# Latent attention of a two-block transformer kernel: keys before queries, and a per-row scale in the exponential

## The reference, cut to what matters

```python
lat = h @ w_in
cq, ckv, k_pe = jnp.split(lat, [Q_LORA, Q_LORA + KV_LORA], axis=-1)
q = (rmsnorm_2(cq, q_norm) @ w_q_up).reshape(B, S, N_HEADS_2, QK_HEAD)
kv = (rmsnorm_2(ckv, kv_norm) @ w_kv_up).reshape(B, S, N_HEADS_2, QK_NOPE + V_HEAD)
k_nope, v = jnp.split(kv, [QK_NOPE], axis=-1)
k = jnp.concatenate([k_nope, jnp.broadcast_to(k_pe[:, :, None, :], ...)], axis=-1)
q = rope_tail(rmsnorm_2(q, q_head_norm), cos, sin)
k = rope_tail(rmsnorm_2(k, k_head_norm), cos, sin)
o = causal_attention(q, k, v)        # softmax(q k^T * QK_HEAD ** -0.5) v
return o.reshape(B, S, N_HEADS_2 * V_HEAD) @ w_out
```

## Time and profile before

| what | value |
|---|---|
| median of the runs | 2693.09 us (2692.44 to 2696.33, three runs) |
| profiled execution, its own time | 2700.57 us |
| its span in the profile | 2698.5 us |
| mean granted TensorE clock | 0.959 |
| latent attention stage, strip 2 to the output strips | 2042.1 to 2290.3 us of the span |

### The profile page before, as it was taken

One profiled execution on the slowest core, in us unless ns is written; L12 is line 12 of the kernel. 1 busy time (PEld: TensorE's weight loads), 2 busy tenths in 40 slices (PEclk: granted clock), 3 DMA queues, 4 the chain that ended last, 5 costly groups with the idle time before them and its releaser, 6 DMA issues.

```text
span 2698.5 us, 29334 instructions
## 1 busy us (share of the span) xinstructions
PE 2587.5 (96%) x10854; PEld 1803.9 (67%) x10854; DVE 1172.3 (43%) x1789; ACT 750.1 (28%) x1049; POOL 29.1 (1%) x24
## 2 busy tenths in 40 slices
PE   7989969999999699999999999999999999999999
PEld 2865533333333488888888888888887646888887
DVE  5765451222221644433644433544436546544432
ACT  3124321000101333322433322333223225433321
POOL 0000000000000300000000000000000000000000
PEclk9986879999999799999899999999999979999999
DMA  6650138999998133322232322333322200233332
GB/s 241 212 171 1 66 137 353 422 422 422 422 422 368 48 100 93 110 100 82 68 98 96 108 96 84 93 101 96 107 85 84 81 32 1 86 101 93 100 106 74
DMA packets 80858, 403.58 MB, mean 150 GB/s; under 512 B 8984, under 2 KB 9496, under 8 KB 55968
## 3 DMA queue, kind: packets, MB, share of 16 engines
q1 hardware_dynamic: 80800, 402.82, 40.8%
HBM read 400.69 MB, written 2.10 MB: 149 GB/s over the span
## 4 chain that ended last, share of the span: by engine, by line
PE 89%; DVE 5%; DMA 2%; ACT 2%; issue 1%; POOL 0%; SPq 0%; ACTq 0%; DVEq 0%; POOLq 0%
PE pb L900 21%; PE pb L901 20%; PE pb L902 20%; PE pb L1108 8%; PE pb L1134 4%; PE pb L1074 2%; PE pb L1095 2%; DMA stage<-in_w_in 1%; PE pb L996 1%; PE pb L1291 1%; PE pb L1009 1%; PE pb L1023 1%; PE pb L997 1%; DMA adaw<-in_w_ada 1%; PE pb L1281 1%
## 5 line engine op out<-in xcount | busy, mean ns | idle before, releaser
L1385 DVE TENSOR_TENSOR wL<-stage,wH 128x1024 fp32r<-128x1024 f32 (+2 forms) x303 | 393.6, 1300 | 821.2 <-ACT wH L539 821.1
L900 PE MATMUL pb<-hH,wH 128*128 128x512 f32 x1688 | 667.8, 396 | 25.7 <-DVE gf L1747 8.5
L901 PE MATMUL pb<-hL,wH 128*128 128x512 f32 x1688 | 660.2, 391 | 0.0
L902 PE MATMUL pb<-hH,wL 128*128 128x512 f32 x1688 | 659.8, 391 | 0.0
L539 ACT ACTIVATE wH<-stage 128x1024 fp32r<-128x1024 f32 (+2 forms) x303 | 337.3, 1114 | 892.5 <-PE pb L902 822.5
L900 PEld LDWEIGHTS pb<-hH,wH 128*128 128x128 f32 x1688 | 319.2, 189 | 103.8 <-issue 11.8
L901 PEld LDWEIGHTS pb<-hL,wH 128*128 128x128 f32 x1688 | 318.9, 189 | 67.6 <-issue 2.8
L902 PEld LDWEIGHTS pb<-hH,wL 128*128 128x128 f32 x1688 | 318.8, 189 | 67.4
L900 PE MATMUL pb<-gH,wH 128*128 128x512 f32 x704 | 273.9, 389 | 0.0
L901 PE MATMUL pb<-gL,wH 128*128 128x512 f32 x704 | 273.9, 389 | 0.0
L902 PE MATMUL pb<-gH,wL 128*128 128x512 f32 x704 | 273.9, 389 | 0.0
(11 more groups left out here) (271 smaller groups left out, 2271.5 us busy)
## 6 DMA issues: line engine op xcount, KB each, us to landing
ring<-in_experts SPq DMA_DIRECT2D x192, 1024.0 KB, 17.7
stage<-in_gate SPq DMA_DIRECT2D x88, 512.0 KB, 3.5
stage<-in_up SPq DMA_DIRECT2D x88, 512.0 KB, 3.5
stage<-in_down SPq DMA_DIRECT2D x64, 704.0 KB, 4.0
adaw<-in_w_ada SPq DMA_DIRECT2D x48, 512.0 KB, 5.5
stage<-in_w_in SPq DMA_DIRECT2D x18, 512.0 KB, 6.7
stage<-in_mla_in SPq DMA_DIRECT2D x9, 512.0 KB, 3.6
stage<-in_q_up SPq DMA_DIRECT2D x12, 384.0 KB, 3.0
```

The costliest lines, as they stand in the source:

```text
L900: pe.matmul(ps, lh, rh, start=first, stop=False)
L901: pe.matmul(ps, lh, rl, start=False, stop=False)
L902: return pe.matmul(ps, ll, rh, start=False, stop=last)
L1385: dve.tensor_tensor(wL[:, n % 2, 0:w], stage[:, n % STAGE, 0:w], wH[:, n % 2, 0:w], ALU.subtract).then_inc(strip_lo, 1)
```

## The change

It touches the latent attention stage only.

- **Order.** Latent strips come as key/value 6, 7, rotated key part 8, then query 0 to 5. Key strips come next, then the twelve query strips (rotated ones at places 0, 1, 6 and 7), then the value strips.
- **Query norms.** A query tile is no longer multiplied by any reciprocal. DVE copies plain tiles and multiplies rotated ones by their gain alone. The sums of squares of the raw queries go to four rows for heads 0 to 3 and 4 to 7, are copied out, turned by 4 small transposes (4 x 128 to 128 x 4), and joined on tokens x heads with the query latent's reciprocal (another 4 transposes): a table of 128 x 32 scales. The exponential takes a column of it as its scale, and the bias is the maximum times the same column.
- **Spreads.** Only the eight for keys are left; two follow each of query strips 3 to 6. Head sums follow each key head and each query strip, rotations 1 to 4 follow query strips 7 to 10. The gain of the queries' plain part is folded into the keys'.
- **Values** are made and taken in the four banks one by one, rather than by waiting for a whole strip.
- **Other.** Angles are worked out in two pieces at strips 2 and 3; the first strip of the output waits for each head's low half in turn, not for all; the second output strip's `hi` and `lo` move into the attention's first units; positions and the selection table are loaded after the fifth latent strip; semaphores, tile counters and banks are renumbered.

The diff, cut to its core:

```diff
-        NX, NCTX, NH2, NFIN, N1A, NMA, N2A, N1B, NMB, NQL, NKL, N2B = range(12)
+        NX, NCTX, NH2, NFIN, N1A, NMA, N2A, N1B, NMB, NKL, NQL, N2B = range(12)
+        LAT_ORDER = (6, 7, 8, 0, 1, 2, 3, 4, 5)
+        Q_ORDER = (0, 1, 4, 5, 6, 7, 2, 3, 8, 9, 10, 11)
+        K_BANKS = ((1, 3, bank(T_MIN + 7), bank(T_MIN + 8)), (1, 3, 7, 6))
+        V_BANKS = (1, 3, bank(T_MQ + 10), bank(T_MQ + 11))
+        def q_scale(h, b):
+            c = 32 + 16 * (h // 4) + 4 * b + h % 4
+            return qstat[:, c:c + 1]
...
# PE
-            for s in range(9):
-                whole(M_IN + s, T_MIN + s, KD, hH, hL, lows_of=LO0[NMB] if s == 0 else None)
-                if s == 0:
-                    norm_sum(NMB)
-                if s == KQ:
-                    norm_sum(NQL)
+            for j in range(9):
+                whole(M_IN + j, T_MIN + j, KD, hH, hL, lows_of=LO0[NMB] if j == 0 else None)
+                if j == 0:
+                    norm_sum(NMB)
+                if j == 3:
+                    norm_sum(NKL)
...
+            def head_sum(n):
+                pe.wait_ge(hq_sq, n + 1)
+                ...
+                if n == 9:
+                    pe.wait_ge(std_done, NQL + 1)
...
+            def qsum_turn(group):
+                pe.wait_ge(qsum_copied, group + 1)
+                for b in range(NB):
+                    mm = pe.transpose(pb[4 + group][:, 4 * b:4 * b + 4], qsum[group][:, b * P:(b + 1) * P], tab("ident", 4)[0:4, :])
+                if group == 0:
+                    pe.wait_ge(rstd_done, NQL + 1)
+                    for b in range(NB):
+                        mm = pe.transpose(pb[4][:, 16 + b:17 + b], rstd_q[0:1, b * P:(b + 1) * P], tab("ident", 1)[0:1, :])
+                mm.then_inc(qsum_turned, 1)
+
+            for m in range(4):
+                keys_of(0, m)
+            turn(0, krope[:, :])
+            head_sum(0)
+            for m in range(4):
+                keys_of(1, m)
+                head_sum(1 + m)
             for s in range(12):
...
+                queries(s)
+                if s < 2:
+                    head_sum(5 + 2 * s)
+                    head_sum(6 + 2 * s)
+                else:
+                    head_sum(7 + s)
+                if s == 1:
+                    norm_sum(NQL, at=4)
+                if 3 <= s <= 6:
+                    spread_rows(2 * s - 6)
+                    spread_rows(2 * s - 5)
+                if 7 <= s <= 10:
+                    turn(s - 6, qr[:, s - 7, :])
+                if s == 9:
+                    qsum_turn(0)
+            head_sum(19)
+            values_of(0, 0)
+            head_sum(20)
+            for i in range(1, 4):
+                values_of(0, i)
+            for i in range(4):
+                values_of(1, i)
+                if i == 1:
+                    qsum_turn(1)
...
-            pe.wait_ge(att_lo, NB + MH)
             for s in range(KD):
-                whole(M_OUT + s, T_MOUT + s, KD, oH, oL)
+                whole(M_OUT + s, T_MOUT + s, KD, oH, oL, heads_of=NB if s == 0 else None)
...
# ACT
             for s in range(12):
                 hi(M_Q + s + 2)
+                if s == 2:
+                    root(NQL, KQ * P, at=4)
+                    act.wait_ge(hq_summed, 9)
+                    act.activation(head_std[:, :], pb[5][0:MH, :], ACT.Sqrt, bias=eps[0:MH, 0:1], scale=1.0 / (NOPE + ROPE))\
+                       .then_inc(hq_std, 1)
...
-                act.activation(p, p, ACT.Exp, bias=stat[:, 16 + u % 4:17 + u % 4], scale=SCALE2,
+                act.activation(p, p, ACT.Exp, bias=stat[:, 16 + u % 4:17 + u % 4], scale=q_scale(h, b),
...
+                if u == 2:
+                    hi(M_OUT + 1)
...
# DVE
+                if s in Q_ROPE:
+                    dve.tensor_scalar(qr[:, Q_ROPE[s], :], ps, col("qh_rope"), None, ALU.mult).then_inc(out_taken, 1)
+                else:
+                    dve.tensor_copy(qn[:, Q_NOPE[s], :], ps).then_inc(out_taken, 1)
+                if 3 <= s <= 6:
...
+                    head_scale(2 * s - 6)
+                    head_scale(2 * s - 5)
...
-                dve.tensor_scalar(stat[:, 16 + u % 4:17 + u % 4], m2, -SCALE2, None, ALU.mult).then_inc(bias_ready, 1)
+                dve.tensor_scalar(stat[:, 16 + u % 4:17 + u % 4], m2, q_scale(h, b), -1.0, ALU.mult, ALU.mult).then_inc(bias_ready, 1)
...
+                if u == 3:
+                    lo(M_OUT + 1)
```

More of the change, by code:

```diff
@@ new lines, in qstat_root @@
+            def qstat_root(group):
+                act.wait_ge(qstat_step, 6 + 5 * group)
+                act.activation(qstat[:, 8:24], qstat[:, 8:24], ACT.Sqrt, bias=eps[:, 0:1], scale=1.0 / (NOPE + ROPE))\
+                   .then_inc(qstat_std, 1)
+            head_square(0, lat[:, 8, :])
+            for h in range(4):
+                key_out(h)
+            hi(M_Q)
+            key_out(4)
+            key_out(5)
+            hi(M_Q + 1)
+            key_out(6)
+            key_out(7)
@@ L865, in soft @@
+                if s == 8:
+                    qsum_out(0)
+                act.wait_ge(out_taken, T_MQ + s + 1)
+                head_square(9 + s, pb[bank(T_MQ + s)][:, :] if s in Q_ROPE else qn[:, Q_NOPE[s], :])
+            qstat_root(0)
+            value_out(0)
+            value_out(1)
+            qsum_out(1)
+            value_out(2)
+            value_out(3)
+            hi(M_OUT)
+            for r in range(4, 8):
+                value_out(r)
+            qstat_root(1)
             def soft(u):
@@ L913, in norm_sum, with whole @@
                     pe.wait_ge(ones_set, 2)
-                pe.matmul(pb[6][:, 0:WID[q]], ones[:, :], ssq[:, 0:WID[q]], start=True, stop=True).then_inc(norm_summed, 1)
-            def whole(n, tile, kt, high, low, lows_of=None, c0=0, used=True, at=None, free=None):
+                pe.matmul(pb[at][:, 0:WID[q]], ones[:, :], ssq[:, 0:WID[q]], start=True, stop=True).then_inc(norm_summed, 1)
+            def whole(n, tile, kt, high, low, lows_of=None, heads_of=None):
                 pe.wait_ge(strip_lo, n + 1)
[L919 to L922, removed]
+                pe.wait_ge(out_taken, tile - 1)
                 for k in range(kt):
@@ L925, in whole @@
                         pe.wait_ge(h_lo, lows_of + k + 1)
[L926 to L929, removed]
+                    if heads_of is not None:
+                        pe.wait_ge(att_lo, heads_of + k + 1)
+                    mm = three(pb[bank(tile)][:, :], weights(n, k * P), (high[:, k, :], low[:, k, :]), k == 0, k == kt - 1)
+                mm.then_inc(strip_used, 1)
             def mod_sum(b):
@@ new lines, in queries @@
+            def queries(s):
+                n = M_Q + s
+                pe.wait_ge(strip_lo, n + 1)
+                if s < 2:
+                    pe.wait_ge(keyed, 3 + s)
+                    pe.wait_ge(hq_sq, 4 + s)
+                else:
+                    pe.wait_ge(out_taken, T_MQ + s - 1)
+                    if s - 2 in Q_ROPE:
+                        pe.wait_ge(hq_sq, 8 + s)
+                for k in range(KQ):
+                    if s == 0:
+                        pe.wait_ge(h_lo, LO0[NQL] + k + 1)
+                    mm = three(pb[bank(T_MQ + s)][:, :], weights(n, k * P), (nH[:, k, :], nL[:, k, :]), k == 0, k == KQ - 1)
+                mm.then_inc(strip_used, 1)
@@ new lines, in values_of @@
+            def values_of(g, i):
+                n = M_V + g
+                r = NB * g + i
+                if i == 0:
+                    pe.wait_ge(strip_lo, n + 1)
+                if g:
+                    pe.wait_ge(valued, r - 3)
+                elif i >= 2:
+                    pe.wait_ge(out_taken, T_MQ + 9 + i)
+                for k in range(KKV):
+                    lhs = (nH[:, KQ + k, i * P:(i + 1) * P], nL[:, KQ + k, i * P:(i + 1) * P])
+                    mm = three(pb[V_BANKS[i]][:, :], lhs, weights(n, k * 512, 512), k == 0, k == KKV - 1)
+                mm.then_inc(v_made if i < 3 else strip_used, 1)
@@ new lines, in query_scales @@
+            def query_scales(group):
+                dve.wait_ge(qstat_std, group + 1)
+                dve.reciprocal(qstat[:, 8:24], qstat[:, 8:24]).then_inc(qstat_step, 1)
+                dve.wait_ge(qstat_step, 7 + 5 * group)
+                for b in range(NB):
+                    c = 32 + 16 * group + 4 * b
+                    dve.tensor_scalar(qstat[:, c:c + 4], qstat[:, 8 + 4 * b:12 + 4 * b], qstat[:, b:b + 1], SCALE2, ALU.mult, ALU.mult)\
+                       .then_inc(scale_ready, 1)
```

425 lines of the change are left out of this document (211 added, 214 removed).

## The result

The changed kernel takes 2667.98 us (median; 2664.57 to 2669.28, four runs), the kernel before 2692.77 us in the same comparison (2686.86 to 2696.33, four runs). The ratio is 0.9910 with a 95% interval of 0.9892 to 0.9927. Against the 2693.09 us that stood before the prediction it is 25.1 us less; forecast were 27. The interval stands for a gain of 20 to 29 us, so the whole time bears the forecast out but cannot tell its terms apart.

What follows compares the result with a forecast made beforehand. PE, busy for 96% of the span, was taken as the bound. 25.6 before the first score + 2.0 - 1.6 + 1.3 in attention gave 27.3 us less than 2693.09: 2666 us, range 2658 to 2678.

Steps and rivals of the forecast that it cites:

- first key matmul to first score: Keys, queries and values: 70.8 fp32r, 36.8 fp32, 1.7 transposes, 4.4 pauses, 1.7 clock; 115.4 us, a gain of 25.6.
- pause at head sum 9: At query strip 2 PE waits for ACT's copy, table switch and query latent root: 3.0 us.
- pause at head sum 0: PE waits for ACT's square behind the last six latent tiles: 1.4 us, ends 0 and 3.
- attention: delayed start: First attention units: second output strip's `lo` delays probabilities and late scales the first mask; +1.6 us, ends 0 and 3.
- attention: scale read from a column: Exponential on ACT perhaps a little longer, with PE the bound: zero, ends 0 and +2 us.
- the second fall: By the skill page's rule, each new pause lowers the clock: one fall more than charged, 1.7 us.
- rival 3: Table switch on ACT costs another 1.3 us, pause at query strip 2 becomes 4.3: 2668 us, chance 0.04.
- The cross-check: Key to first score: spreads 10.8, waits 7.2, clock 15.4 make 33.4 us, less 4.4 + 1.7 + 1.7: 25.6.
- Rival 5: Nothing happens, because the spreads lay beside other work: 2693 us, chance 0.01.
- rival 1: Clock falls in the new places too, in the parts with keys and spreads; 10.8 us lost: 2677 us, chance 0.12.
- rival 2: Key part: PE waits for ACT's square and copy of each key head, 5 us in all: 2671 us, chance 0.15.
- rival 4: Slower: whole part from keys to values runs at 1.2 GHz, +108 us: 2773 us, chance 0.02.

Runs made afterwards that it cites:

- experiment 6: Changed kernel with the query latent's root ahead of the copy of query strip 4 on ACT's list: 2658.31 us, stage 216.3 us against 220.9.
- experiment 1: Kernel before with each spread reading 128 rows (120 of them zero) instead of 8: 2685.70 us against 2694.77, ratio 0.9965; stage 237.7 us.
- Experiment 3: Changed kernel with twelve more spreads as repeats: stage 242.4 us with 8 rows (2695.04 us), 230.2 with 128 rows (2675.62 us).
- Experiment 7: Changed kernel with second output strip's copies later and fifth key head in a free bank: 2671.49 us; with the query latent's root moved too: 2663.74 against 2668.32.
- experiment 5: Changed kernel with the old wait for all heads' low halves before the first output strip: 2674.63 us, stage 222.5 us, attention 67.2 instead of 65.5.
- both edits: Kernel before, old order, without the twelve query spreads and with 128 rows in the eight key spreads: 2677.5 us, stage 234.2 us from 248.2.

## Why the prediction was right

| term, us | forecast | measured |
|---|---|---|
| latent strips | 0 | -0.7 |
| first key matmul to first score | 115.4 | 115.3 |
| pause at head sum 9 | 3.0 | 3.08 |
| pause at head sum 0 | 1.4 | 1.37 |
| the clock's fall behind the first pause | 1.7 | 1.5 (experiment 6) |
| attention: full clock at the first scores | -2.0 | -1.85 |
| attention: delayed start | +1.6 | +1.57 |
| attention: scale read from a column | 0 | +0.94 |
| attention: wait before the output strips | -1.3 | -1.65 |
| attention, the four together | -1.7 | -1.0 |
| stage | -27.3 | -27.3 |

**The middle part** held, and in the main for the reason given: what is left of it is PE's own list at the full clock with the two pauses that were forecast. Pricing each fp32 matmul by its neighbours (1.18 for the first, 0.90 for the next) was good to a few tenths. Some of the closeness is luck. The 1.4 us for head sum 0 was borrowed from another wait, no row showed it. The list has 18 groups of fp32 matmuls and not 19, which is 0.3 us too much, and the wait of 0.34 before head sum 20 was not forecast; the two cancel. So do, in the stage, the 0.7 us of the latent strips and the 0.7 by which the attention fell short.

That spreads would not slow the clock in their new places held, but the ground given for it was weak: rotations and head sums, which had held 1.00 between strips, read 128 rows, and experiment 1 shows that this is the difference that counts. Nothing in the rows said that two spreads of 8 rows between strips are few enough. Experiment 3 shows that five are not: they cost 12 us for the clock alone.

**The pages.** "TensorE: Matmul & The Clock Gate" of the Trainium skill (What's actually happening, and HAM oscillation) ties the clock to how busy PE has been. Here the trace disagrees in one kind of work: with PE busy and 8 rows read the clock was at 0.50 at 2178 us, and with 128 rows read it was 1.00 around the same twelve query spreads (experiment 1). For pauses the traces agree in part: the pause of 3.08 us was followed by the only low stretch of the changed stage, and falls followed the pauses of 2.16, 2.09 and 1.66 us in experiment 1; but none followed those of 1.37 and 1.81 us in the changed stage. So the second fall that the prediction worked out for a rule of pauses did not come. The drain that "ScalarE: Activation LUTs" of the Trainium skill (What ACT_TABLE_LOAD costs) puts behind a table load again did not show: the root starts 1.29 us after the load, so rival 3 fell.

**Attention** holds the term that was mis-sized, and it is not the delayed start. PE's lists tell where the time went. In the kernel before, from the first score at 2223.84 us:

```profile
2230.00 0.27 PE L1352 MATMUL pb<-tabs,prob 128*128 128x128 f32 x1
...
2236.16 2.39 PE L1360 MATMUL pb<-pT2a,V 128*128 128x512 f32 x8
...
2286.50 2.42 PE L1360 MATMUL pb<-pT2b,V 128*128 128x512 f32 x8 [0.69 <-ACT pT2b L877]
```

In the changed kernel, whose output strips start at 2259.22 us:

```profile
2193.72 0.38 PE L1445 MATMUL pb<-kn,qn 128*128 128x128 f32 x2
...
2198.03 0.27 PE L1453 MATMUL pb<-tabs,prob 128*128 128x128 f32 x1
...
2205.76 2.42 PE L1461 MATMUL pb<-pT2a,V 128*128 128x512 f32 x8
...
2257.04 2.42 PE L1461 MATMUL pb<-pT2b,V 128*128 128x512 f32 x8 [0.69 <-ACT pT2b L920]
```

- From the first score to the first turned probability the same matmuls take 6.16 us before and 4.31 after: 1.85 for the clock.
- From there to the first product with the values it is 6.16 before and 7.73 after: the delayed start takes back 1.57, as forecast. Experiment 7 splits it: 1.10 go when the moved copies leave the start, and the other 0.47 are left for the late scales and the first, slower exponentials.
- From the first product to the last, seven heads on, it is 50.34 before and 51.28 after. This is the term put at nothing, "ACT is idle for 31 of 66.5 us there, and PE is the bound". PE is the bound, but once a head its product with the values waits for a copy that stands on ACT behind an exponential: at the fourth head it starts 0.06 us after that copy ends, and 0.09 before the change. A head takes 7.79 us where it took 7.64. The chain before that copy has grown by as much: DVE's step that makes the bias takes 0.21 us instead of 0.15, the exponential 0.09 more. No run takes the column away alone, so this cause is read from the lists, not shown by an experiment.
- From the last product to the output strips it is 3.83 before and 2.18 after: 1.65 for the old wait, as in experiment 5.

**The cross-check was right by its sum only.** It gave 15.4 us to the clock, 10.8 to the spreads and 7.2 to the waits, less 7.8; the 3 us that it takes off the low time have no row. Measured alone, the clock of the spreads is worth 10.5 us (DVE, which needs 1.43 us for a key head, sets the pace when PE no longer does), and the twelve spreads 10.8 with their low clock, since 5.6 us of new waits come out from behind them. Both together are 14.0. The other 13.3 us of the 27.3 are the new order's: in the old order with both edits PE still waits for 14.4 us before the first score, in the new one for 4.8; the attention part is 0.9 shorter and the latent one 0.7, and the remaining 2 us or so go, by an estimate, with the lower clock (0.96 against 0.99 before the first score) after the old waits. So neither the removal nor the reordering would have done it alone; the new order with twelve more spreads had a stage of 242.4 us (experiment 3), 5.8 under the old. Rival 5, that the spreads lay beside other work, was false of the old kernel, but had a true core: they did cover something.

Rivals 1, 2 and 4 did not come: no low clock beside the spreads, no wait of a key strip on ACT's copies, 0.99 in the middle part.

## What to carry to other kernels

Count the matmuls that read only a few rows apart from the rest: a run of them can bring the clock down although the engine is never idle, so spread them thinly between full ones, or fill the rows with zeros, which cost no time on TensorE here (587 ns a pass with 8 rows, 590 with 128, at the full clock). Before work is removed from a busy engine, ask which waits it hid, and leave other work of that engine in front of them. Walk each engine's list along the diff: moving one root ahead of a copy on an idle engine gave back a pause of 3.1 us and 1.5 us of clock. And an engine that is idle half the time is not free: if the busy engine waits for it once in a loop, every tenth of a microsecond put on that chain is paid each time round.

## What the runs showed of the hardware that had not been expected

- With 8 rows read in each spread the old third stretch took 73.5 us at a clock of 0.77; with 128 rows and the same list it took 63.2 us at 0.95. In the changed kernel five spreads of 8 rows between strips of 4.08 us gave 0.90 before the first score, two gave 0.99.
- Behind pauses the clock fell in some cases and not in others: it fell after 3.08, 2.16, 2.09 and 1.66 us, and did not after 1.37 and 1.81 us.
- In a group of five spreads at the full clock the first takes 0.96 us from start to start and each further one 0.86, whether it repeats the one before or goes on to the next head (2133.22, 2134.08 and 2134.94 us in experiment 3 with 128 rows). The prediction had 0.90. That twelve of them added only 0.78 each to the stage is not explained by these steps.
- The exponential with its scale read from a column takes longer by 91 to 94 ns at every width. The rows of the kernel before and of the changed one (min/median/max in ns):

```profile
L869 ACT ACTIVATE prob<-prob,stat x32: 402/562/722, 2225.6 to 2283.0; 128x128 f32<-128x128 f32 x8, 128x256 f32<-128x256 f32 x8, 128x384 f32<-128x384 f32 x8, 128x512 f32<-128x512 f32 x8
```

```profile
L912 ACT ACTIVATE prob<-prob,stat,qstat x32: 493/653/816, 2196.1 to 2253.5; 128x128 f32<-128x128 f32 x8, 128x256 f32<-128x256 f32 x8, 128x384 f32<-128x384 f32 x8, 128x512 f32<-128x512 f32 x8
```

  Over 32 units that is 3 us of ACT's time. Most of it is hidden behind PE, but about 0.15 us a head is not, together with DVE's longer step for the bias (0.21 us instead of 0.15).
